# Attention probabilities scaled before they are transposed, one output accumulation per query tile, and scores issued earlier, in a two-layer RG-LRU and sparse-attention trunk

## The reference

```python
p = jax.nn.softmax(s, axis=-1)            # per branch; s causal, scaled
o = einsum(p, v)                          # per branch
y_nsa = gates[..., 0:1] * o_cmp + gates[..., 1:2] * o_slc + gates[..., 2:3] * o_win
y = concatenate([y_lru * silu(g_lru), y_nsa * silu(g_nsa)])
return x + y @ w_out                      # per layer; rmsnorm at the end
```

## Time and profile before

| | us |
|---|---|
| median of 3 runs | 619.94 (619.82 to 620.29) |
| the profiled execution, in the same measure | 621.83 |
| its span in the trace, first to last instruction | 620.1 |
| PE busy | 582.4 |
| DVE busy | 402.8 |
| ACT busy | 293.9 |
| mean granted clock of TensorE | 0.986 |

### The profile page before, as it was taken

How to read it: one execution, slowest core, us unless ns; L and a number is a source line. 1 busy time by engine, 2 the same in 40 slices (tenths; PEclk the granted TensorE clock), 3 DMA queues, 4 the chain that set the end, 5 groups by cost and what they waited for, 6 DMA issues and landing times.

```text
span 620.1 us, 8688 instructions
## 1 busy us (share of the span) xinstructions
PE 582.4 (94%) x3207; PEld 408.2 (66%) x3207; DVE 402.8 (65%) x690; ACT 293.9 (47%) x586; POOL 40.0 (6%) x80
## 2 busy tenths in 40 slices
PE   4999999989999989998999999999999999999985
PEld 3777767777656555555888686877776666555654
DVE  4786967886555654755476689678765676566531
ACT  3647654525444543542453664462444545444421
POOL 1001101210000000000230110102000000000000
PEclk9999999999999998999899999999999999999997
DMA  8756393444111110101232755735321220000112
GB/s 244 202 159 156 87 227 93 89 99 127 35 35 35 35 34 1 35 0 35 68 103 73 193 142 143 139 81 116 101 69 35 69 49 20 2 1 1 35 34 69
DMA packets 94121, 50.71 MB, mean 82 GB/s; under 512 B 42992, under 2 KB 92288, under 8 KB 94080
## 3 DMA queue, kind: packets, MB, share of 16 engines
q1 hardware_dynamic: 91456, 45.95, 29.5%
q0 software_dynamic: 1536, 3.15, 2.1%
q10 hardware_dynamic: 1088, 1.06, 0.6%
HBM read 44.90 MB, written 2.10 MB: 76 GB/s over the span
## 4 chain that ended last, share of the span: by engine, by line
PE 65%; DVE 17%; ACT 8%; issue 5%; DMA 3%; POOL 1%; POOLq 0%; DVEq 0%; ACTq 0%
PE z_ps L1351 10%; PE z_ps L1353 9%; PE z_ps L1352 9%; PE s_ps L1410 7%; PE t_ps L1426 6%; PE a_ps L1462 5%; PE o_ps L1462 3%; DVE w_lo L983 3%; DMA swp<-E 2%; ACT probs L928 2%; PE s_ps L1413 2%; PE o_ps L1351 2%; PE o_ps L1353 2%; PE o_ps L1352 2%; DVE probs L1157 2%
## 5 line engine op out<-in xcount | busy, mean ns | idle before, releaser
L1351 PE MATMUL z_ps<-h_hi,w_hi 128*128 128x512 f32 x264 | 111.3, 421 | 3.2 <-DVE h_lo L976 2.3
L928 ACT ACTIVATE probs<-s_ps,mn 128x128 f32<-128x128 f32 (+3 forms) x128 | 66.3, 523 | 100.0 <-DVE mn L1259 87.8
L1352 PE MATMUL z_ps<-h_lo,w_hi 128*128 128x512 f32 x264 | 103.6, 393 | 0.0
L1353 PE MATMUL z_ps<-h_hi,w_lo 128*128 128x512 f32 x264 | 103.6, 392 | 0.0
L785 ACT ACTIVATE w_hi<-stage 128x1024 fp32r<-128x1024 f32 x58 | 61.1, 1054 | 75.0 <-PE z_ps L1353 46.0
L1259 DVE TENSOR_REDUCE mn<-s_ps 128x1 f32<-128x128 f32 (+3 forms) x128 | 56.8, 485 | 51.6 <-PE s_ps L1413 51.4
L983 DVE TENSOR_TENSOR w_lo<-stage,w_hi 128x1024 fp32r<-128x1024 f32 x58 | 71.1, 1226 | 11.3 <-ACT w_hi L785 10.0
L1351 PEld LDWEIGHTS z_ps<-h_hi,w_hi 128*128 128x128 f32 x264 | 49.9, 189 | 22.4 <-issue 14.5
L1353 PEld LDWEIGHTS z_ps<-h_hi,w_lo 128*128 128x128 f32 x264 | 49.8, 189 | 11.0
L1267 DVE COPY probsT<-t_ps 128x512 f32<-128x512 f32 (+1 forms) x48 | 33.0, 687 | 35.9 <-PE t_ps L1426 24.8
L1352 PEld LDWEIGHTS z_ps<-h_lo,w_hi 128*128 128x128 f32 x264 | 50.1, 190 | 7.8 <-issue 0.2
...
## 6 DMA issues: line engine op xcount, KB each, us to landing
...
```

The costliest lines, as they stand in the source:

```text
L928: act.activation(probs[:, 4 * (u % 2) + j, 0:W], s_ps[g][:, 0:W], ACT.Exp, scale=-1.0, bias=mn[:, u % 2, j:j + 1], accum_out=rs[:, b, col: ...
L1351: pe.matmul(bank, w_hi[:, slot, at:at + P], x_hi, start=first, stop=False)
L1352: pe.matmul(bank, w_hi[:, slot, at:at + P], x_lo, start=False, stop=False)
L1353: ins = pe.matmul(bank, w_lo[:, slot, at:at + P], x_hi, start=False, stop=last)
```

## The change

Probabilities are scaled before they are transposed. A new step N, one per unit, waits for the unit's four exps; DVE makes the reciprocal of the four row sums and multiplies by the gates, then scales the rows of two heads in place; ACT waits for the coefficients and scales the rows of the other two. The first T of a unit waits for both, where it waited for the exps. K, B and O go. The three branches of a query tile now add up in one bank: o_ps and a_ps alternate by query tile, and the first W of tile i waits for Y of tile i - 2. Y reads the bank. probsT has four data buffers instead of three and one for coefficients. In `attention`, the two S of the next unit move from 0.2 and 0.6 to 0.0 and 0.4, N stands at 0.9, and Y, YH and YL come sooner after the last W of a tile.

```diff
-N_STAGE, N_RING, N_PT, N_E, N_SWP = 4, 3, 3, 6, 2
+N_STAGE, N_RING, N_PT, N_E, N_SWP = 4, 3, 4, 6, 2
...
-            due.setdefault(n + 2, []).append(("YH", l, "n", i))
-            due.setdefault(n + 5, []).append(("YL", l, "n", i))
+            due.setdefault(n + 1, []).append(("YH", l, "n", i))
+            due.setdefault(n + 3, []).append(("YL", l, "n", i))
...
-                if st[0] == "W" and st[2][0] == "P" and st[2][3:] == (1, st[2][1]):
-                    _, i, b, _, _ = st[2]
-                    due.setdefault(n + 1 + b, []).append(("T", l, ("B", i, b)))
-                    due.setdefault(n + 4 + 2 * b, []).append(("O", l, i, b))
-                    if b == 1:
-                        waiting.append((n + 9, i))
-                if st[0] == "W" and st[2][0] == "C" and st[2][2] == 1:
-                    due.setdefault(n + 3, []).append(("O", l, st[2][1], 2))
+                if st[0] == "W" and st[2][0] == "P" and st[2][2:] == (1, 1, st[2][1]):
+                    waiting.append((n + 2, st[2][1]))
...
-                   [("CS2", l)], *fill(per_unit[-1] - 2)])
+                   [("N", l, units[0])], [("CS2", l)], *fill(per_unit[-1] - 2)])
...
-            if k == 0 and pair == 1:
-                main[-1].append(("K", l, i, b))
...
-        s += flat_list(weave(main, (ahead, 0.0, 0.8), (fill(per_unit[u]), 0.0, 1.0)))
+        norm = [[("N", l, units[u + 1])]] if u + 1 < len(units) else []
+        s += flat_list(weave(main, (ahead, -0.2, 0.6), (fill(per_unit[u]), 0.0, 1.0), (norm, 0.8, 1.0)))
...
-        def o_bank(l, i, b):
-
-            return o_banks[group_no[(l, i, b)] % 2]
+        def o_bank(l, i):
+
+            return o_banks[(TT * l + i) % 2]
...
+                elif kind == "N":
+                    _, l, unit = st
+                    u, W = unit_no[(l, *unit)], P * (unit[0] + 1)
+                    act.wait_ge(coef_ok, u + 1)
+                    for j in (2, 3):
+                        rows = probs[:, 4 * (u % 2) + j, 0:W]
+                        ins = act.activation(rows, rows, ACT.Copy, scale=coef[:, u % 2, j:j + 1])
+                    ins.then_inc(norm_act, 1)
...
+                    dve.wait_ge(exp_ok, 4 * (u + 1))
+                    link(dve.reciprocal(coef[:, u % 2, :], rs[:, u % 2, :]))
...
+                    dve.tensor_tensor(c4, c4, gate, ALU.mult).then_inc(coef_ok, 1)
+                    dve.wait_ge(coef_ok, u + 1)
+                    for j in (0, 1):
+                        rows = probs[:, 4 * (u % 2) + j, 0:W]
+                        ins = dve.tensor_scalar(rows, rows, coef[:, u % 2, j:j + 1], None, ALU.mult)
+                    ins.then_inc(norm_dve, 1)
...
-                    dve.wait_ge(o_done, group_no[(l, i, 1)] + 1)
-                    dve.scalar_tensor_tensor(out=e, in0=e, scalar=0.5, in1=silu_g[:, :, i * P:(i + 1) * P],
-                                             op0=ALU.mult, op1=ALU.mult).then_inc(ynsa_ok, 1)
+                    dve.wait_ge(pv_done, turn_no[(l, "P", i, 1, 1, i)] + 1)
+                    wait_e((l, f"y{i}"))
+                    dve.scalar_tensor_tensor(out=e, in0=o_bank(l, i)[:, :].rearrange("p (r q) -> p r q", r=GROUP), scalar=0.5,
+                                             in1=silu_g[:, :, i * P:(i + 1) * P], op0=ALU.mult, op1=ALU.mult).then_inc(ynsa_ok, 1)
...
-                        pe.wait_ge(exp_ok, 4 * (u + 1))
+                        pe.wait_ge(norm_dve, u + 1)
+                        pe.wait_ge(norm_act, u + 1)
...
-                    for r in range(GROUP):
-                        ins = pe.transpose(bank[:, r * P:(r + 1) * P], wide_c[:, r * P:(r + 1) * P], ident[:, :])
...
-                first = pair == 0 and k == 0
-                group = group_no[(l, i, b)]
-                if first and group >= 2:
-                    pe.wait_ge(o_done, group - 1)
+                first, last = (b, pair, k) == (0, 0, 0), (b, pair, k) == (1, 1, i)
+                if first and TT * l + i >= 2:
+                    pe.wait_ge(ynsa_ok, TT * l + i - 1)
```

More of the change, by code:

```diff
@@ L301, in __init__ @@
                 self.e.append(st[1:])
-            elif k == "O" and st[3] == 0:
+            elif k == "Y":
                 self.e.append((st[1], f"y{st[2]}"))
@@ L336, in __init__ @@
         self.turn_no = {key: n for n, key in enumerate(self.turns)}
-        self.data = [key for key in self.turns if key[1] != "B"]
-        self.data_no = {key: n for n, key in enumerate(self.data)}
-        self.groups = [st[1:] for st in sched if st[0] == "O"]
-        self.group_no = {key: n for n, key in enumerate(self.groups)}
-        self.coefs = [st[1:] for st in sched if st[0] == "K"]
-        self.coef_no = {key: n for n, key in enumerate(self.coefs)}
         self.silus = {key: n for n, key in enumerate(st[1:] for st in sched if st[0] == "SG")}
@@ L401, in hybrid_trunk @@
         probs = sb("probs", [P, 8, SEQ])
-        probsT = sb("probsT", [P, N_PT + 1, SEQ])
+        probsT = sb("probsT", [P, N_PT, SEQ])
         q_st = sb("q_st", [P, 8, SEQ], F32R)
@@ L438, in hybrid_trunk @@
         dump = [E[:, 2:4, :], E[:, 4:6, :], silu_g[:, 0:2, :], silu_g[:, 2:4, :]]
-        sq_tmp, sq_acc, spread_c = swp[:, 0, :], upad[:, CONV_W - 1:], upad[:, CONV_W - 1:]
+        sq_tmp, sq_acc = swp[:, 0, :], upad[:, CONV_W - 1:]
         diag = probs[:, 0, :]
@@ L443, in hybrid_trunk @@
         THR, THI, TH, SQ = (probsT[:, n, :] for n in range(4))
-        wide_c = probsT[:, N_PT, :]
         yn_hi, yn_lo = q_st[:, 0:GROUP, :], q_st[:, GROUP:2 * GROUP, :]
@@ L921, in _ @@
                             act.wait_ge(t_full, turn_no[(old[0], "P", *old[1:], old[1])] + 1)
-                        if pair == 0 and (i >= 1 or l >= 1):
-                            act.wait_ge(coef_ok, plan.coef_no[(l, i - 1, b) if i >= 1 else (l - 1, TT - 1, b)] + 1)
                     for g in range(N_KV):
@@ L1261, in _ @@
                     key = (st[1], *st[2])
[L1262 to L1263 removed]
+                    n, rows = turn_no[key], P if key[1] == "P" else NC
+                    if n % 2 == 1:
                         dve.wait_ge(t_full, n + 1)
[L1265 to L1291 removed]
@@ new lines, in _ @@
+                        if n >= N_PT:
+                            dve.wait_ge(pv_done, n - N_PT + 1)
+                        dve.tensor_copy(probsT[0:rows, n % N_PT, :], t_ps[n % 2][0:rows, :]).then_inc(pt_dve, 1)
+                elif kind == "N":
+                    _, l, unit = st
+                    i, b, pair = unit
+                    u, W = unit_no[(l, *unit)], P * (i + 1)
+                    dve.wait_ge(exp_ok, 4 * (u + 1))
+                    link(dve.reciprocal(coef[:, u % 2, :], rs[:, u % 2, :]))
+                    gate = gates[:, i, :].rearrange("p (g r b) -> p b g r", g=N_KV, b=3)[:, 1 + b, :, 2 * pair:2 * pair + 2]
+                    c4 = coef[:, u % 2, :].rearrange("p (g r) -> p g r", g=N_KV)
+                    dve.tensor_tensor(c4, c4, gate, ALU.mult).then_inc(coef_ok, 1)
[4 more added lines that the diff above has]
+                    ins.then_inc(norm_dve, 1)
@@ L1444, in weigh @@
                     _, _, i, b, pair, k = key
-                    last = pair == 1 and k == i
                 else:
                     _, _, i, pair = key
-                    b, k, last = 2, 0, pair == 1
-                first = pair == 0 and k == 0
-                group = group_no[(l, i, b)]
-                if first and group >= 2:
-                    pe.wait_ge(o_done, group - 1)
-                if first and group - per_layer(plan.groups, l) < 2:
+                    b, k = 2, 0
+                first, last = (b, pair, k) == (0, 0, 0), (b, pair, k) == (1, 1, i)
+                if first and TT * l + i >= 2:
+                    pe.wait_ge(ynsa_ok, TT * l + i - 1)
+                if first and i < 2:
                     pe.wait_ge(z_dve, plan.freed(plan.z, z_no[("Z", l, LAST)])[1])
@@ L1460, in weigh @@
                         v, rows = vc_sb[:, g, :], NC
-                    ins = pe.matmul(o_bank(l, i, b)[g * HD:(g + 1) * HD, pair * N_PAIR_COL:(pair + 1) * N_PAIR_COL], v,
-                                    probsT[0:rows, d % N_PT, g * 2 * P:(g + 1) * 2 * P],
+                    ins = pe.matmul(o_bank(l, i)[g * HD:(g + 1) * HD, pair * N_PAIR_COL:(pair + 1) * N_PAIR_COL], v,
+                                    probsT[0:rows, n % N_PT, g * 2 * P:(g + 1) * 2 * P],
                                     start=first, stop=last, skip_group_check=True)
```

82 lines of the change are left out of this document (18 added, 64 removed).

## The result

The changed kernel is slower: 629.53 us (median of 4 runs, 626.92 to 631.69) against 620.12 (619.82 to 621.55) for the kernel before on the same chip, a ratio of 1.0159 (95% interval 1.0127 to 1.0191), so slower by more than the noise, though by less than 2%. Forecast were 613.0 us, at most 621. The profiled execution took 626.92 us, its span is 625.1; before it was 620.1.

The account below looks back on a forecast made before the run. PE, busy 94% of the span, was taken as the bound. Savings of 25.3 us less 18.3 us of new waits and clock loss gave net 7.0 us: span 613.1, median 613.0, range 603 to 621.

Parts of the forecast that it names:

- What goes: Savings from removed PE steps, both layer tails, waits for upad with slow clock, and waits for exp: 25.3 us.
- B: PE's transposes of the coefficients, 16 in two layers at 0.43 us, nothing hiding them: removal saves 6.9 us.
- Both tails: PE's waits for the last y split ending each layer, and the clock loss behind, go: 4.8 and 5.3 us.
- The waits for upad: Branch C's second T waiting for ACT's coefficient copy: 2.1 + 1.1 us go, plus 3.2 us of slow clock.
- The second S: Waits of a unit's second S for the exp of the first: 1.9 of 3.4 us go, 1.5 stay.
- N, layer 0: PE's waits for scaled rows at units' first T in layer 0, mostly behind evictions on DVE: 11.1 us.
- N, layer 1: The same waits in layer 1, mostly covered by more pieces per unit: 0.2, 0.3 and 0.8 us.
- W for copies: W waits until ACT finishes the next unit's exps and the copy of the first T: 3.4 us.
- Clock: One fall of PE's clock, behind the 2.3 us wait for scaled rows at layer 0's unit (2, 0, 0): 2.5 us.
- The sign set for a wrong forecast: Waits for probs under 6 or over 16 us, or low clock in several slices of layer 0's attention.
- Rival 2: The clock falls at layer 0's eight waits for N, 3.2 us each, giving 636 us; chance 0.13.
- Rival 3: Queues on ACT and DVE: layer 0's waits for N and W grow by half, 7 us, giving 620; chance 0.16.

Follow-up runs that it names:

- e9: The kernel before with short tails in both layers and without B and its copy on ScalarE (scaling of y wrong): 601.78 us, ratio 0.9729.
- e1: The kernel before with only the tails shortened: B, O, Y, YH and YL follow the last W of either layer sooner; 610.01 us, ratio 0.9853.
- e12: The changed kernel with N put ahead of GE at two places of layer 1, units (3, 1, 0) and (3, 1, 1): 622.89 us, ratio 1.0087.
- e3: The changed kernel with the two S of the next unit back at 0.2 and 0.6 of a unit: 657.51 us, ratio 1.0617.
- e5: e4 with ScalarE copying a transposed tile before the exps where T directly follows S and the copy is ScalarE's: 609.01 us, ratio 0.9814.
- e4: The changed kernel with N put ahead of the evictions and y splits directly in front of it, at ten places: 613.28 us, ratio 0.9912.

## Why the prediction was wrong, step by step

**What goes, 25.3 us.** Held, nearly all of it. B: 6.9 forecast, 8.3 by the balance, 8.4 by e9. Both tails: no wait for q_st is left in the changed kernel, and e1 shows 5.9 of 6.7 us of waits and the clock behind them by themselves. The waits for upad went (3.2 us). But the 3.2 us of clock set down to the long one did not follow from that wait: e1 has the wait without the fall. The sum took as certain what one execution showed and another did not. The second S: forecast 1.5 us of 3.4 to stay, measured 5.2. Of these 2.2 are the one behind N and CS2, where 0.9 was expected: N delays CS2, CS2 delays the minima.

**N, layer 0: 11.1 us.** Measured 7.7. Unit by unit the count was good: (0, 0, 1) 1.3 against 1.5, (1, 0, 1) 1.5 against 1.7, (1, 1, 1) 1.3 against 1.5, (2, 0, 0) 2.0 against 2.3, (0, 1, 1) 0.5 against 0.7, (3, 0, 0) 0.8 against 1.2. (3, 1, 0) did not wait (0.5), and the three units without an eviction in front, 1.7 us in the sum, waited 0.4.

**N, layer 1: 1.3 us. This step failed.** Measured 7.0, of which 4.2 at two T, (3, 1, 0) with 1.6 and (3, 1, 1) with 2.7. The steps weighed cover against the chain, and evictions only in layer 0. Layer 1 has an eviction of another kind, GE, whose operation on VectorE waits for one on ScalarE: 1.4 us ahead of N, not 0.7. In the order of the end of layer 1 (shown ahead of the prediction) L1314 was in view, for the tails; its place next to N wasn't looked up. e12 shows that it was worth 4.5 us. That all waits for N came to 14.7 us, inside the 6 to 16 that the prediction allowed, is luck: layer 0 was counted 3.4 us too high and layer 1 5.7 too low.

**W for copies: 3.4 us. This step failed too.** Measured 10.0, where the kernel before had 1.4, so 8.6 came. The prediction counted an exp pair ahead of the copy only where the cover was short, from exp and copy times alone. What it left out is that the exps themselves wait for the minima, with ScalarE idle (1.62 us in the rows above), and the copy behind them. e3 (2.6 us with S further back) and e5 (3.6 us with the copy first) show the cause from both sides.

**The whole distance.** Forecast were 7.0 us less of span, measured 5.0 more. Against the sum, copies are 5.2 us worse, S for exps 3.7, N 2.1 (14.7 less the 0.2 of before, against 12.4), the clock 2.4, and PE's work 1.4 better (8.3 for 6.9): 12.0. The other 4.5 us between 613.0 and 629.5 lie between span and median: the median is 1.9 us below the profiled execution before, and 2.6 above it in the changed kernel. By layers, the waits for N, copies and exps are 18.2 us in layer 0 (1.6 of them there before as well), where 15.2 were counted, and 11.7 in layer 1, where 2.1 were. So most of the miss is layer 1, called covered because PE has more pieces there.

**Clock: 2.5 us.** Measured 5.1 in the profiled execution, three stretches of 1.7, and up to 5 us more in the other runs by their spans. They stand behind waits of 2.2 us (S for exps), 1.96 (W for a copy) and 2.7 (N, in layer 1), but not behind that of 1.98 us at (2, 0, 0), the one the prediction named:

```profile
218.48 0.63 PE L1395 MATMUL t_ps<-ident,probs 128*128 128x128 f32 x4 [1.98 <-ACT probs L926]
...
215.00:224.00 9.00, 6.83 (x46) 4.12 (x44) 6.06 (x14) 5.25 (x14) 0.00 (x0) 1.00 0.00 1
```

The sign set for a wrong forecast, low clock in more than one slice of layer 0's attention, came. Rival 2 did not: no fall in layer 0 stands behind a wait for N in this execution. In e3, where five such waits of layer 0 took 2.0 to 2.9 us, the clock fell at four of them (not at 270.57), and once more at a wait of 1.1 us (292.87). The Trainium skill (TensorE: Matmul & The Clock Gate, the section on HAM oscillation) has a loop that falls at every wait, and the prediction gave rival 2 its time by that. That loop's waits, 3 to 5 us by the page, are longer than any wait for N here, so the rule was stretched. Here the trace agrees in part: with 22 waits for N in e3 the clock fell in ten stretches and took 20.4 us, in e4 twice.

**The rivals.** Rival 3, queues on ACT and DVE, named the right kind of cause, in the wrong place. It let N and W grow by half in layer 0; there they waited 14.1 us, with 13.7 counted. The excess is in the N and W of layer 1 (10.6 against 2.1) and in S for exps. Its size, 7 us at most, was less than the 11.0 us of waits that came over the sum: it was a share of the waits already counted, and so could not hold the ones that the count had missed. With N ahead of the evictions the same change gives 613.3 us, which is the forecast's number by coincidence, by a different sum: N 3.1, copies 11.5, exps 5.5.

**Small terms.** The scalings on ScalarE, forecast at 0.40 to 0.72 us, are 0.395 to 0.714:

```profile
L926 ACT ACTIVATE probs<-probs,coef 128x512 f32<-128x512 f32 x16 | 10.7, 714 | 8.3 <-DVE coef L1253 8.1
...
L926 ACT ACTIVATE probs<-probs,coef 128x128 f32<-128x128 f32 x16 | 5.6, 395 | 11.3 <-DVE coef L1253 11.3
```

The Trainium skill (VectorE: DVE Perf Modes, the section on the TRN2 errata) gives 224 cycles plus one per column at 1.2 GHz; an estimate from that is 0.29 and 0.61 us. Both rows are 0.10 above it, and its slope agrees. The busy times came as forecast (VectorE 401.8, ScalarE 315.2).

**Open.** Why one wait makes the clock fall and an equal one doesn't, and why it stays low for 4, 8 or 18 us, no run here tells. The fourth buffer of probsT, the single accumulation per tile and the earlier Y were not varied by themselves; of the waits of PE in the changed kernel none over 0.2 us is for a bank that Y has to free.
